# Moving the first convolution tap to ScalarE, and the last S5 quad's four products to TensorE sums

## What is computed

```
state = associative_scan(a, bu)                         # complex, 64 states per group, 32 groups
y = real(einsum("ghp,blgp->blgh", c_mat, state))        # = c_re * re(state) - c_im * im(state)
y = y + d_skip * u ;  z = gelu(y) @ w_glu
```

```
qk = silu(conv_depthwise(concat(q, k), w, b))           # y[t] = w0 x[t-3] + w1 x[t-2] + w2 x[t-1] + w3 x[t] + b
```

## Time and profile before

| | us |
|---|---|
| median of 3 runs | 1402.83 |
| lowest, highest | 1401.02, 1409.48 |
| profiled execution | 1403.95 |
| its span in the trace | 1402.2 |

### The profile page before, as it was taken

One profiled execution on the slowest core, in us unless ns is written; L12 is line 12 of the kernel. 1 busy time (PEld: TensorE's weight loads), 2 busy tenths in 40 slices (PEclk: granted clock), 3 DMA queues, 4 the chain that ended last, 5 costly groups with the idle time before them and its releaser, 6 DMA issues.

```text
span 1402.2 us, 14197 instructions
## 1 busy us (share of the span) xinstructions
PE 1215.9 (87%) x4476; PEld 654.3 (47%) x4476; DVE 875.5 (62%) x1760; ACT 415.1 (30%) x1128; POOL 510.4 (36%) x579
## 2 busy tenths in 40 slices
PE   7999988889678778676689877779999999999997
PEld 2675555444244322222245532237444444999443
DVE  2667668554753555666656656769989652766445
ACT  2213343324232343243433343423212511222000
POOL 1000356556656656666666666620011100000000
PEclk9999999999899989899889989999999999999999
DMA  9999789989989999999999999966343424444440
GB/s 345 334 386 328 294 304 349 341 296 369 370 301 341 391 402 396 355 382 363 355 365 357 360 359 380 368 234 240 121 169 130 164 91 171 170 154 168 180 180 30
DMA packets 131851, 399.41 MB, mean 285 GB/s; under 512 B 10413, under 2 KB 11821, under 8 KB 131520
## 3 DMA queue, kind: packets, MB, share of 16 engines
q0 software_dynamic: 74448, 271.09, 51.9%
q1 hardware_dynamic: 55604, 123.29, 24.4%
q10 hardware_dynamic: 1724, 4.13, 0.8%
HBM read 397.42 MB, written 1.05 MB: 284 GB/s over the span
## 4 chain that ended last, share of the span: by engine, by line
PE 45%; issue 29%; POOL 10%; DMA 5%; DVE 4%; SPq 2%; another core or an unknown queue 2%; DVEq 1%; ACT 1%; POOLq 0%; ACTq 0%
PE psum L730 21%; PE psum L1377 6%; PE psum L1416 6%; POOL gathered L639 5%; POOL gathered L653 5%; PE psum L1069 2%; DMA gathered<-in_peer_u_dram,expert_idx 2%; DVE gathered L2341 2%; DMA work<-in_meta_tokens_dram 2%; PE psum L851 2%; DMA gathered<-in_peer_v_dram,expert_idx 2%; PE psum L753 1%; DVEq L2343 1%; SPq L573 1%
## 5 line engine op out<-in xcount | busy, mean ns | idle before, releaser
L1069 PE MATMUL psum<-gathered,modr 128*128 128x512 f32 x1024 | 516.4, 646 | 155.0 <-issue 66.4
L2341 DVE CUSTOM_DVE_ANT_0 gathered<-gathered,psum 128x1024 f32<-128x1024 f32 x256 | 311.5, 1217 | 211.0 <-DMA gathered<-in_peer_u_dram,expert_idx 190.1
L1069 PEld LDWEIGHTS psum<-gathered,modr 128*128 128x128 f32 x1024 | 195.2, 203 | 445.6 <-issue 346.0
L639 POOL DMA_INDIRECT gathered<-in_peer_u_dram,expert_idx x256 | 243.7, 952 | 248.8 <-DVE expert_idx L1894 147.4
L653 POOL DMA_INDIRECT gathered<-in_peer_v_dram,expert_idx x256 | 242.4, 947 | 182.7 <-remote 67.6
L730 PE MATMUL psum<-weight_ring,featT 128*128 128x512 f32 x368 | 162.0, 596 | 1.2 <-ACT featT L1468 0.8
L730 PE MATMUL psum<-featT,weight_ring 128*128 128x128 f32 (+2 forms) x832 | 126.0, 306 | 7.1 <-issue 6.8
L730 PEld LDWEIGHTS psum<-featT,weight_ring 128*128 128x128 f32 x832 | 116.1, 195 | 29.2 <-issue 23.9
L1635 ACT ACTIVATE gel<-dots 128x1 f32<-128x1 f32 x256 | 50.4, 197 | 213.6 <-issue 107.8
L730 PEld LDWEIGHTS psum<-weight_ring,featT 128*128 128x128 f32 x368 | 68.6, 190 | 87.1 <-issue 84.9
L1644 ACT ACTIVATE modr<-ident,wgt 128x128 f32<-128x128 f32 x256 | 102.8, 402 | 21.2 <-issue 3.8
(11 more groups left out here) (424 smaller groups left out, 1342.8 us busy)
## 6 DMA issues: line engine op xcount, KB each, us to landing
weight_ring<-in_w_in_dram SPq DMA_DIRECT2D x14, 2048.0 KB, 11.1
weight_ring<-in_w_up_dram SPq DMA_DIRECT2D x8, 2048.0 KB, 8.5
weight_ring<-in_w_down_dram SPq DMA_DIRECT2D x8, 2048.0 KB, 7.8
weight_ring<-in_ada_w_dram SPq DMA_DIRECT2D x6, 2048.0 KB, 18.0
work<-in_ada_w_dram SPq DMA_DIRECT2D x5, 2048.0 KB, 15.0
weight_ring<-in_peer_wq_dram SPq DMA_DIRECT2D x3, 2048.0 KB, 12.5
gathered<-in_peer_u_dram,expert_idx POOLq DMA_INDIRECT x256
gathered<-in_peer_v_dram,expert_idx POOLq DMA_INDIRECT x256
```

What stands on the lines that cost most here:

```text
L639: pool.indirect_dma_start(u_rows[:, slot, :], None, T["peer_u"], bass.IndirectOffsetOnAxis(ap=expert_idx[:, r % 2, k:k + 1], axis=0),).the ...
L1069: mm = pe.matmul(psum[:, SUM_BANK + half, :], diag[:, e % 8, :], v_rows[:, slot, 512 * half:512 * (half + 1)], start=(e % EXPERTS == 0), s ...
L2341: dve.tensor_tensor_reduce(u_rows[:, slot, :], u_rows[:, slot, :], h2_rows[t], 1.0, 0.0, ALU.mult, ALU.add, dots[:, col:col + 1])
```

## The change

1. In quad 3 only, VectorE makes −sin·zi in place of sin·zi (one `scalar_tensor_tensor`), the other two products are written in place, and the two sums are gone. `s5_out(3)` makes four calls for each of its four places in place of two, and PSUM adds them up.
2. The 8 instructions of the first tap go from VectorE to ScalarE as scaled Copies, behind the small Exp and ahead of `gelu_y(3)`. VectorE waits for a new flag `first_tap` ahead of `s5_y(3)`.

```diff
                 pe.wait_ge(flag("state_ready"), q + 1)
+                parts = ((0, 2), (1, 3)) if q < 3 else ((0, 2), (0, 3), (1, 4), (1, 5))
                 for i in range(4):
-                    for c in range(2):
+                    for j, (c, s) in enumerate(parts):
                         last = pe.matmul(psum[32 * i:32 * i + 32, 6, 0:SEQ], cd[:, c, 4 * q + i, :],
-                                         s5t[2 + c][:, i, META:LEN], start=(c == 0), stop=(c == 1))
+                                         s5t[s][:, i, META:LEN], start=(j == 0), stop=(j == len(parts) - 1))
                 last.then_inc(flag("y_full"), 1)
...
             act.activation(enm, gcol[:, 3 * MH:5 * MH], ACT.Exp, scale=-1.0).then_inc(flag("enm"), 1)
+            for m in range(8):
+                last = act.activation(qkT[:, m, :], qk_in[:, m, 0:LEN], ACT.Copy,
+                                      scale=pk("qk_w")[:, m:m + 1])
+            last.then_inc(flag("first_tap"), 1)
             gelu_y(3)
             act.wait_ge(flag("conv2_y"), 1)
...
                 tt(a, cos, zr, ALU.mult)
-                tt(b, sin, zi, ALU.mult)
-                dve.drain()
+                if q == 3:
+                    stt(b, sin, -1.0, zi, ALU.mult, ALU.mult)
+                else:
+                    tt(b, sin, zi, ALU.mult)
+                dve.drain()
+                if q == 3:
+                    tt(zi, cos, zi, ALU.mult)
+                    tt(zr, sin, zr, ALU.mult).then_inc(flag("state_ready"), 1)
+                    return
                 tt(a, a, b, ALU.subtract)
...
             w = pk("qk_w").rearrange("p (k m) -> p k m", k=4)
-            for m in range(8):
-                ts(qkT[:, m, :], qk_in[:, m, 0:LEN], w[:, 0, m:m + 1])
+            dve.wait_ge(flag("first_tap"), 1)
             s5_y(3)
             for k in range(1, 4):
```

## The result

| | before | changed |
|---|---|---|
| median of 20 runs | 1409.04 us | 1415.99 us |
| lowest, highest | 1397.08, 1417.87 | 1408.11, 1430.3 |
| profiled execution | 1403.95 | 1416.55 |
| its span | 1402.2 | 1414.8 |

The ratio is 1.0054, with an interval of 1.0031 to 1.0077: slower by 7.6 us, between 4.4 and 10.8. (The medians in the table differ by 6.95 us; the ratio leaves out the one slow run of the changed kernel, 1430.3 us.) The forecast was 3.8 us more than before, 1406.6 us, with a range of 1402.3 to 1411.0; the measured 1415.99 us lies outside. The three runs of before that were shown ahead had a median of 1402.83; over 20 runs it is 1409.04.

What follows compares the result with a forecast made beforehand. TensorE's own program was taken to bound the stretch; 3.0 us from the late read of gm 3 plus 0.8 from GpSimd's addition gave 1402.83 + 3.8 = 1406.6 us, range 1402.3 to 1411.0.

Steps and rivals of the forecast that it cites:

- TensorE's products: `s5_out(3)`: 8 more calls, 16 more records at 64 ns, delay gm 2, the broadcasts and gm 3 by 1.02 us.
- Rival 6: `s5_out(3)`: the four-call sum on TensorE doesn't overlap and costs several us; about +4.5 us, 1407.3; chance 3%.
- The 1.02 us lie inside this wait: Before glu: TensorE idles 2.7 us for ScalarE's read of gm 3, so the extra products' 1.02 us aren't added.
- The first tap: Eight taps on ScalarE take 3.5 us; VectorE's other 24 start 4.2 us late, and glu starts 3.0 us late.
- rival 5: ScalarE: one table load more for the Copies behind the Exp, 1.28 us; +5.1 us, 1407.9; chance 5%.
- VectorE's quad 3: Two sums fewer save 2.6 us, the `scalar_tensor_tensor` takes 1.29 us; worth nothing, as TensorE asks for the state later.
- Rival 3: VectorE's path, 5.7 us shorter, removes TensorE's two waits, 0.75 and 0.77 us; faster, 1401.3; chance 4%.
- GpSimd's addition: Third addition starts 0.4 us ahead of VectorE's three limits and holds them up; the TensorE delay grows 0.8 to 3.8 us.
- Rival 1: Only the wait before glu counts: VectorE's limits start before GpSimd's addition or don't wait for it; +3.0 us, 1405.8; chance 25%.
- TensorE's clock: A rival: after idling before glu, the granted clock falls to 0.50, costing 1.8 us; +5.6 us, 1408.4; chance 10%.
- the base: Whole kernel: median of the runs before taken as 1402.83 us, moving by 2 us or so; the forecast was added to it.

Runs made afterwards that it cites:

- o1_order: The changed kernel with the 16 calls turned, all four places for one product before the next; calls 1.93 us, stretch 60.88 us, ratio 1.0038 against before.
- t2_taps_again: Second run of the kernel before with only the first tap moved to ScalarE, S5 part as before; stretch 60.89 us, no ratio.
- e1_early_taps: Kernel before with the first tap on ScalarE behind gelu_y(2), and s5_y(3) ahead of the last tap; stretch 57.01 us, ratio 0.9999.
- op_both: `o1_order` with GpSimd's third addition made to wait for E_args; limits 1.23 us, stretch 59.93 us, ratio 1.0033 against the kernel before.
- s1_s5_only: The changed kernel with the first tap kept on VectorE, so only the S5 part changes; stretch 60.51 us, ratio 1.0027 against before.
- t1_taps_only: Kernel before with only the first tap moved to ScalarE, S5 part as before; stretch 61.62 us, ratio 1.0051 against before.
- o2_pairs: The changed kernel with the 16 calls in pairs, two products for each place in turn; calls 1.98 us, stretch 61.62 us, no ratio.
- n1_null: The kernel before, unchanged, timed against itself; stretch 57.02 us, ratio 1.0002.

## Why the prediction was wrong, and where it was right

**TensorE's products: the term that was mis-sized.** The step was "8 calls more are 16 records more: 16 x 64 ns = 1.02 us". They cost 3.50 us. I scaled a row that was made of overlapping calls, and gave an end only below, none above. Two lengths in the trace of before would have given the upper end: 4 calls of one per place took 0.57 us and 8 of two per place 1.02. That is 0.45 us for a second call in every place (0.42 for each further one in `o1_order`), so 16 calls without any overlap would take 16 x 0.43 = 6.9 us. That the 8 took 1.02 us showed that they overlapped, and I didn't ask what order lets them. Rival 6 named the right mechanism, had 3%, and its figure of +4.5 us was near the measured +4.2.

**"The 1.02 us lie inside this wait."** With 3.5 us they don't: gm 3 ends later than ScalarE can read it, and TensorE sets glu's start at +3.51 in place of +3.0. The error in the term was 2.5 us, in the stretch only 0.3, because ScalarE's lateness stood beside it (61.20 against the 60.88 of `o1_order`).

**The first tap: right.** Taps on ScalarE 3.39 us (3.5 forecast), second tap 4.2 us late (4.2), Silus likewise. Shown alone by `t2_taps_again` and with TensorE's part cheap by `o1_order`, where +3.87 stands against the forecast's 3.8. The estimate of 3.4 us for the eight that the prediction worked out from the figures of the Trainium skill (ScalarE: Activation LUTs, "What ACT_TABLE_LOAD costs") was nearer than mine. No table load more was needed for them (rival 5).

**VectorE's quad 3: right and worth nothing.** The `scalar_tensor_tensor` took 1.29 us, and the quad ended 2.7 us earlier than before, counted from the stretch's start (2.6 forecast); VectorE then idled for 10.78 us. Rival 3, the gain of 5.7 us on VectorE, is excluded by `e1_early_taps`.

**GpSimd's addition: right in kind.** In `o1_order` it starts at 1015.85, 0.38 us ahead of the limits (0.4 forecast), and they take 5.21. In the changed kernel it starts 0.21 behind the first of them, gets in behind the second and holds up the third; the delay of `E_args` is the same to 0.4 us. That a `tensor_scalar` waits for GpSimd, which no row of before showed, is shown by `op_both`. The trace agrees with the rule of the Trainium skill (SBUF — State Buffer, "SBUF: two separate sides") that whoever starts first has the shared ports for the whole instruction. Rival 1, without this race, would be about +3.5 on the changed kernel, an estimate from `s1_s5_only`; it was not run.

**TensorE's clock: possible, not the cause.** It stayed at 1.00 in the three profiles of the changed kernel in this stretch.

**The absolute time and the range: the base was mis-sized.** The measured 1416.0 us is 9.4 above the forecast. The largest part is the base: the range stood on three runs of before, for which I allowed "2 us or so", and their median was 6.2 us below that of twenty. The stretch adds 0.4 us (4.2 in place of 3.8). The other 2.8 us lie ahead of the stretch, and no run ties them to the change. In ratio, the forecast's 1.0027 is what two of three comparisons measured, 1.0027 and 1.0025, with a stretch of +4.2 us; the first measured twice that.

## What to carry to other kernels

When a row is scaled by a count, ask first whether it was made of overlapping pieces, and price the addition from both sides: alone, and fully overlapped. Where calls on TensorE go to several places of 32 columns, as here, turn the loops so that at most two in a row go to one place. And before work is moved to an idle engine, find the instruction that it will stand behind in that engine's program: idle time on average was no help to taps that could not begin until the consumer already wanted them.

## What the runs showed of the hardware that was not expected

- Calls of 128x32 by 128x256 in float32 for four places of 32 columns overlap as long as at most two in a row have the same place: 16 calls took 1.93 us in single turns, 1.98 in pairs, 3.30 in threes and 4.59 in fours.
- VectorE's `tensor_scalar` with immediate operands from SBUF to SBUF and GpSimd's addition exclude each other both ways. Three limits took 1.23 us alone and 5.2 behind its start; the addition took 4.50 us where it started first, and 4.71 (before) and 5.05 (changed) where a limit was already running. The twelve that read PSUM took 4.67 us in every kernel, but the addition ran beside them for 0.3 us at most, so whether they would wait isn't shown.
- Behind waits of 2.8 to 3.7 us with TensorE busy ahead of them, the granted clock fell to 0.50 in two profiles of five (`t1_taps_only`, `o2_pairs`; not in `t2_taps_again`, `o1_order`, `op_both`), at the price of 1.7 us. The same wait of 3.69 us went both ways.
- The same kernel takes 1409 us in one series and 1322 in the others, with a mean granted clock of 0.958 and 0.988 in their profiles. All of the difference lies ahead of the stretch (1046.55 against 964.55 in `n1_null`), in the expert stage, where the DMA engines moved the same bytes, at 357 GB/s over 776 us and at 399 over 694. What makes it slower was not asked.
